# Inverting the heads' triangular matrices as 32x32 blocks: four packed levels and one corner level instead of five 64x64 levels

## The reference

```
def step(state, inp):
    r_t, w_t, k_t, v_t, a_t, b_t = inp
    sa = jnp.einsum('bhvk,bhk->bhv', state, a_t)
    state = state * w_t[:, :, None, :] + sa[..., None] * b_t[:, :, None, :] + v_t[..., None] * k_t[:, :, None, :]
    y = jnp.einsum('bhvk,bhk->bhv', state, r_t)
    return state, y
```

## Time and profile before

| | |
|---|---|
| Median of 3 runs | 3258.43 us (3256.69 to 3261.16) |
| Span of the profiled execution, first to last instruction | 3254.1 us, 4.3 us under the median |
| Stage of the heads, in that span | from about 2330 to 2832 us |
| Its 8 merges | 25.5 to 26.9 us each |
| PE busy over the span | 3029.2 us, 93% |

### The profile page before, as it was taken

How to read it: one execution, slowest core, us unless ns; L and a number is a source line. 1 busy time by engine, 2 the same in 40 slices (tenths; PEclk the granted TensorE clock), 3 DMA queues, 4 the chain that set the end, 5 groups by cost and what they waited for, 6 DMA issues and landing times. The chain is left out here.

```text
span 3254.1 us, 59877 instructions
## 1 busy us (share of the span) xinstructions
PE 3029.2 (93%) x25454; PEld 2407.3 (74%) x25454; DVE 1840.2 (57%) x2665; ACT 1393.4 (43%) x2369; POOL 669.5 (21%) x542
## 2 busy tenths in 40 slices
PE   8989999999978999999989999989788989699999
PEld 6757788887746788887658888767577777588887
DVE  6665533445665543445665736474376867457464
ACT  5555322235455422234464424345465655344242
POOL 1000311211000311212001101133275746011010
PEclk9989999999999999999999999989899999899999
DMA  4101333222101322322012323235411111133232
GB/s 148 52 2 67 103 97 97 92 96 84 52 5 64 99 95 94 97 94 77 1 53 92 109 84 101 88 107 192 142 48 30 49 36 42 48 97 108 80 98 83
DMA packets 82344, 260.72 MB, mean 80 GB/s; under 512 B 9632, under 2 KB 13216, under 8 KB 81824
## 3 DMA queue, kind: packets, MB, share of 16 engines
q1 hardware_dynamic: 71424, 235.39, 22.6%
q10 hardware_dynamic: 10656, 21.50, 1.7%
HBM read 235.89 MB, written 20.97 MB: 79 GB/s over the span
## 5 line engine op out<-in xcount | busy, mean ns | idle before, releaser
L1696 DVE TENSOR_TENSOR mlp_w_lo<-mlp_ring,mlp_w_hi 128x1024 fp32r<-128x1024 f32 (+1 forms) x211 | 251.7, 1193 | 576.8 <-ACT mlp_w_hi L1673 576.7
L1673 ACT ACTIVATE mlp_w_hi<-mlp_ring 128x1024 fp32r<-128x1024 f32 (+1 forms) x211 | 213.2, 1011 | 646.1 <-PE ps L1634 639.2
L1696 DVE TENSOR_TENSOR ffn_w_lo<-ffn_ring,ffn_w_hi 128x1024 fp32r<-128x1024 f32 (+3 forms) x172 | 224.1, 1303 | 443.0 <-ACT ffn_w_hi L1673 443.0
L1673 ACT ACTIVATE ffn_w_hi<-ffn_ring 128x1024 fp32r<-128x1024 f32 (+3 forms) x172 | 187.2, 1089 | 485.9 <-PE ps L1634 480.2
L1633 PE MATMUL ps<-mlp_more_parts,mlp_w_hi 128*128 128x512 f32 x952 | 373.1, 392 | 0.0
L1632 PE MATMUL ps<-tiles_parts,mlp_w_hi 128*128 128x512 f32 x832 | 329.7, 396 | 1.1 <-issue 1.1
L1632 PE MATMUL ps<-ffn_x_parts,ffn_w_hi 128*128 128x512 f32 x792 | 312.4, 395 | 17.8 <-DVE ffn_x_parts L2411 14.2
L1634 PE MATMUL ps<-tiles_parts,mlp_w_lo 128*128 128x512 f32 x832 | 327.7, 394 | 0.0
L1632 PE MATMUL ps<-mlp_more_parts,mlp_w_hi 128*128 128x512 f32 x760 | 305.4, 402 | 21.0 <-DVE mlp_w_lo L1696 12.6
L1633 PE MATMUL ps<-ffn_x_parts,ffn_w_hi 128*128 128x512 f32 x792 | 309.9, 391 | 0.0
L1634 PE MATMUL ps<-ffn_x_parts,ffn_w_lo 128*128 128x512 f32 x792 | 309.9, 391 | 0.0
(11 more groups left out here) (504 smaller groups left out, 6166.2 us busy)
## 6 DMA issues: line engine op xcount, KB each, us to landing
ffn_ring<-in_w_ffn_up SPq DMA_DIRECT2D x88, 512.0 KB, 3.5
mlp_ring<-in_w_up SPq DMA_DIRECT2D x64, 512.0 KB, 3.6
mlp_ring<-in_w_down SPq DMA_DIRECT2D x64, 512.0 KB, 3.5
rwkv_keep<-ffn_ring ACTq DMA_DIRECT2D x64, 256.0 KB, 2.4
sq<-rwkv_keep SPq DMA_DIRECT2D x64, 256.0 KB, 3.1
ffn_ring<-in_w_ffn_down SPq DMA_DIRECT2D x16, 768.0 KB, 4.3
in_ring<-in_w_in SPq DMA_DIRECT2D x22, 512.0 KB, 3.6
mlp_ring<-in_w_in SPq DMA_DIRECT2D x22, 512.0 KB, 3.5
```

The lines of the kernel that those rows point to most:

```text
L1673: nc.scalar.activation(w.w_hi[:, n % SPLIT, 0:width], w.ring[:, n % RING, 0:width], ACT.Copy).then_inc(s["w_hi_ready"], 1)
L1696: nc.vector.tensor_tensor(w.w_lo[:, n % SPLIT, 0:width], w.ring[:, n % RING, 0:width], w.w_hi[:, n % SPLIT, 0:width].bitcast(F32), ALU.sub ...
```

## The change

A 64x64 triangular matrix is cut into two 32x32 diagonal blocks and the 32x32 corner between them. The four first levels work on the diagonal blocks alone. A block's 32 columns are the same columns of the buffers for both blocks, so that `X`, `XT`, `T1` and `NM` are 32 columns wide for each instance (128x128 for each `t`, before 128x256). For that `gram_a` writes rows 32 to 63 of each chunk with their column halves exchanged (`swapped`), so that the own block always stands in columns 0 to 31 of `M0` and the corner of the odd rows in columns 32 to 63. Each of the four levels has `inner` and `outer` of 16 matmul calls of 32x32 instead of 8 of 64x64. The fifth level is one 32x32 corner for each chunk and instance: 8 calls of 32x32 for `inner`, straight from `M0`, and 8 for `outer`. A new buffer `XF` of full width takes the result: POOL puts the diagonal blocks into it (`place`, with a mask), and ACT copies the corner into it in two instructions. `wt` and `u0` read `XF`. The half of `gram_a` that makes `M0` has 16 calls with 32 columns of weights instead of 8 with 64. POOL makes a `part` for four levels instead of five, on 128x128.

```diff
+BW = HD // 2
-RW_LEVELS = 5
+RW_LEVELS = 4
...
-    for level in range(RW_LEVELS):
+    for level in range(RW_LEVELS + 1):
         for tt in range(2):
             order.append((tt, level, False))
...
-        X = sb("X", [P, NT, 4, HD])
-        XT = sb("XT", [P, NT, 4, HD])
-        T1 = sb("T1", [P, 2, 4, HD])
-        NM = sb("NM", [P, PARTS_AHEAD, 4, HD])
+        X = sb("X", [P, NT, 4, BW])
+        XT = sb("XT", [P, NT, 4, BW])
+        XF = sb("XF", [P, NT, 4, HD])
+        T1 = sb("T1", [P, 2, 4, BW])
+        NM = sb("NM", [P, PARTS_AHEAD, 4, BW])
...
-                    for k in range(2):
-                        for d in range(2):
+                    for d in range(2):
+                        for odd in range(2):
                             for hh, u in diagonals():
...
+                                own = slice(at.start + odd * BW, at.start + (odd + 1) * BW)
+                                rhs = BK[lo, c % 2, 0, d, at]
+                                nc.tensor.matmul(m.ps[on, 4 + hh, packed(d)], A[lo, d, own], swapped(rhs) if odd else rhs, start=True, stop=True,
+                                                 skip_group_check=True)
...
                     for i in range(4):
-                        for chunk in (half(0), half(1)):
-                            mm = nc.tensor.matmul(m.ps[chunk, t % 2, packed(i)], NM[chunk, u % PARTS_AHEAD, i, :], XT[chunk, t, i, :],
+                        if level == RW_LEVELS:
+                            for chunk in range(2):
+                                odd = block_of(chunk, 1)
+                                mm = nc.tensor.matmul(m.ps[block_of(chunk, 0), t % 2, narrow(i)], M0[odd, t, i, BW:HD], XT[odd, t, i, :],
+                                                      start=True, stop=True, skip_group_check=True)
+                            continue
+                        for b in range(4):
+                            on = narrow(b)
+                            mm = nc.tensor.matmul(m.ps[on, t % 2, narrow(i)], NM[on, n % PARTS_AHEAD, i, :], XT[on, t, i, :],
                                                   start=True, stop=True, skip_group_check=True)
...
+                        for b in range(4):
+                            on = narrow(b)
+                            mm = nc.tensor.matmul(m.ps[on, 2 + t, narrow(i)], X[on, t, i, :], T1[on, t % 2, i, :],
                                                   start=False, stop=True, skip_group_check=True)
...
+                    act.wait_ge(s["placed"], 4 * c + t + 1)
+                    for chunk in range(2):
+                        on = block_of(chunk, 0)
+                        nc.scalar.activation(XF[on, t, :, BW:HD], m.ps[on, 2 + t, narrow(4, 4)].rearrange("p (i n) -> p i n", i=4), ACT.Copy).then_inc(s["xf_taken"], 1)
...
+                def place(c, t):
+                    pool.wait_ge(s["xt_taken"], within(c, t, RW_LEVELS - 1) + 1)
+                    own = XT[:, t, :, :].unsqueeze(2).broadcast_to([P, 4, 2, BW])
+                    where = mask("place").rearrange("p (h n) -> p h n", h=2).unsqueeze(1).broadcast_to([P, 4, 2, BW])
+                    nc.gpsimd.tensor_tensor(XF[:, t, :, :].rearrange("p i (h n) -> p i h n", h=2), own, where, ALU.mult).then_inc(s["placed"], 1)
```

More of the change, by code:

```diff
@@ L72 @@
 BANDS2_W = 3 * P
-RMASKS, RMASKS_W = columns(("after", HD), ("before", HD), ("upto", HD), ("pair", HD), ("eye", HD), ("merge", RW_LEVELS * HD))
+RMASKS, RMASKS_W = columns(("after", HD), ("before", HD), ("upto", HD), ("place", HD), ("pair", BW), ("eye", BW), ("merge", RW_LEVELS * BW))
 def constants():
@@ L121, in table @@
     def table(name, ones, level=0):
-        r[:, RMASKS[name] + level * HD:RMASKS[name] + (level + 1) * HD] = ones
-    table("after", i > j)
+        width = ones.shape[1]
+        r[:, RMASKS[name] + level * width:RMASKS[name] + (level + 1) * width] = ones
     table("before", i < j)
     table("upto", i <= j)
+    odd, other = i // BW == 1, j // BW == 1
+    table("place", odd == other)
+    i, j = i % BW, j % BW
+    table("after", np.where(other, odd, i > j))
+    j = j[:, :BW]
     table("pair", (i // 2 == j // 2) & (i > j))
@@ L2636, in unit, with within @@
             return 20 * c + 4 * level + t
+        def within(c, t, level):
+            return 16 * c + 4 * level + t
         iterations = range(-1, DT + 2)
@@ L2801, in seed @@
                         pe.wait_ge(s["bonus_ready"], c + 1)
[L2802 removed]
+                    nc.tensor.matmul(m.ps[:, 2 + t, narrow(0, 4)], m.ident, flat(XT[:, t, :, :]), start=True, stop=True).then_inc(s["seeded"], 1)
                 def inner(c, t, level):
[L2805 to L2806 removed]
+                    u, n = unit(c, t, level), within(c, t, level)
+                    if level < RW_LEVELS:
+                        pe.wait_ge(s["nm_ready"], n + 1)
                     if level == 0 and t == 0:
@@ L3132, in _ @@
                             x0(i, t)
-                    parts = [(t, level) for _, t, level, second in merge_order() if not second]
+                    parts = [(t, level) for _, t, level, second in merge_order() if not second and level < RW_LEVELS]
                     for t, level in parts[:PARTS_EARLY]:
@@ L3137, in _ @@
                     parts = iter(parts[PARTS_EARLY:])
-                    for k, _, _, second in merge_order():
+                    for k, t, level, second in merge_order():
                         more = None if second else next(parts, None)
@@ L3141, in _ @@
                             part(i, *more)
+                        if main and level == RW_LEVELS and not second:
+                            place(i, t)
                         scale_beat(i + 1, k)
@@ L3172, in x_turned @@
                 def x_turned(c, t, level):
-                    dve.wait_ge(s["xt_taken"], unit(c, t, level) + 1)
+                    dve.wait_ge(s["xt_taken"], within(c, t, level) + 1)
                     nc.vector.transpose(flat(X[:, t, :, :]), flat(XT[:, t, :, :])).then_inc(s["x_turned"], 1)
@@ L3329, in _ @@
                     for k, t, level, second in merge_order():
-                        if main and second and level < RW_LEVELS - 1:
+                        if main and second and level < RW_LEVELS:
                             x_turned(i, t, level)
```

66 lines of the change are left out of this document (41 added, 25 removed).

## The result

The changed kernel takes 3364.4 us in the median of 4 runs (3360.5 to 3368.2), the kernel before 3257.6 us on the same chip (4 runs, 3253.9 to 3261.2). The ratio is 1.0323, with a 95% interval of 1.031 to 1.0337: some 105 us slower. Forecast were 3339 us within 3300 to 3378, so sign, mechanism and range held, and the size was 25 us short.

A forecast was written before the change was run, and what follows sets the result against it. Instruction supply to PE was taken as the bound: five steady intervals +43.0 us, seventh +10.2, first +8.7, last stretch +11.1, first seeds -0.8, clock +8, together +80 us, giving 3339 us within 3300 to 3378.

The forecast's parts named there:

- The instructions: Merge and gram_a: 1024 + 128 = 1152 more PE instructions an iteration, 4.5 packets; 239 packets in all instead of 203.
- The supply as the bound: PE in the merge waits for its instructions, fed 256 at a time, one such packet in 3.75 us.
- The dense stretch: From the merge's start to the last `turn`: 15.4 packets instead of 10.9, 56.1 us instead of 46.7, +9.4 us.
- The formula: Time from merge start to last `turn`: 14.4 packets at 3.75 us plus one at PE's own 2.1 us, 56.1 us.
- The start with a gain: At the merge's start the instruction buffer is full, so one packet passes at PE's own pace, 2.1 us.
- The clock: Behind the merge, `wt`, `u0` and `sum_outputs` run partly at the lower clock: 1 us an interval (0 to 3), +8 in all.
- The other dense stretches: Outside the five steady intervals: first interval +8.7 us, seventh +10.2, last merge and what follows it +11.1.
- Seeds: Between the last `turn` and the next merge, moving operands fall from 256 to 128 columns: 0.8 us less each time.
- Work inside the stretch: In the merge, a new unit's 32 records start within 0.27 us; PE's savings and 2.3 us of tiling changes are hidden.
- That the supply isn't the bound: Rival: in the merge PE runs ahead and DVE decides, 2.8 us saved a steady iteration, 3231 us; chance 0.04.
- A deeper buffer: Rival: between merges one packet more is buffered, each of 8 stretches 3.75 us shorter, 3309 us; chance 0.10.
- The clock that stays low behind the merge: Rival: the part between last `turn` and next merge is slow too, 6 us of passes double, 3381 us; chance 0.11.

The follow-up runs named there:

- the doses: The changed kernel with 512 more, 512 fewer or 1024 fewer PE instructions an iteration, by adding or leaving out small calls: 3416.9, 3296.7 and 3262.2 us.
- the added calls: The changed kernel with four more one-column 32x32 calls in each inner and outer of levels 0 to 3: 3416.9 us, ratio 1.049.

## Why the prediction was right, and what was off

*The instructions.* Right to the packet: 1152 an iteration, 239 packets.

*The supply as the bound.* Right. The stalls stand 256 instructions apart, the time follows the number of instructions in the doses down to where DVE binds, and neither the columns nor a higher clock changes it. What the runs don't show is why a packet takes so long; the profile has the queue's packets, but not what starts one.

*The dense stretch.* This is the term that was mis-sized. The formula gave 56.1 us. The five steady iterations take 349.83 us (2425.09 to 2774.92), 70.0 each, and 9.6 of it is the sparse stretch with the margins of the earlier trace rows, so 60.4 are left: 4.3 more than forecast.

In the merge (35.1 us by the formula, 37.8 measured) the step that was off is the time of a packet. 3.75 us was called the fastest that PE is fed, but it is the mean of three counts, of 5, 5 and 7 packets in a window, where one packet more or less moves the result by some 0.5 us. Measured from stall to stall, a packet takes 3.90 us, and 4.52 where transfers run. With 4.0, the mean of all 58, the formula gives 2.1 + 8.8 x 4.0 = 37.3 us. The start with a gain was right: up to the end of the first stall the five merges take 3.8 us in the mean for 343 records, 11 ns each, where a packet of 251 in 4.0 us is 16 ns. Waits for DVE or ACT aren't what lengthens a packet: the windows of 4.55 and 4.97 us shown above hold none. They have a DMA share of 0.50 and 0.37, against 0.02 in the shorter ones. The profile counts q8's packets and the transfers' against the same 16 DMA engines, so that the one may well delay the other, but no run moved a transfer, and it stays an association, seen in this run and in the one with 4 columns to move.

Behind the merge the formula has 21.0 us (5.6 packets of 3.75), and 22.6 were measured (the five windows' mean of 22.8, less 0.2 of margin). There the supply isn't the bound: PE is busy for 21.02 of 22.02 us, and the stalls of "issue" are 0 to 1.5 us in such a stretch, 0.7 in the mean of the five. The stretch had 20.4 us before, and `gram_a`'s 8 more calls for each `t` and their changes of tiling run in the open here.

*The clock.* It did fall, to a granted 0.50, the lower of the two levels (1.2 GHz), in most of the merge, and to 0.86 to 0.89 behind it. No run shows the 1 us an iteration that was put down for it there, and none excludes it. Part of the 1.6 us above may be it.

*The other dense stretches.* The first interval grew by 11.8 us (8.7 forecast), the seventh by 12.9 (10.2), the five steady ones by 64.4 (43.0), the last merge and what follows by 17.6 (11.1). Their sum is 106.6; the first merge begins 1.9 us earlier (0.8 forecast), and the spans are 104.6 apart, where the sum had 80 with its 8 for the clock. What follows the last merge grew from 43.26 to 47.53 us, though no instruction was added there. With 4 columns to move it is 45.4, with wide work 45.1. Part of it may be the granted clock of 0.72, against 0.84 in the same stretch before; I leave it open.

*Seeds.* 0.83 us less in the sparse stretch (10.48 to 9.65 above), 0.8 forecast.

*Work inside the stretch.* The small calls started 13.5 ns apart at the lower clock (0.42 us in 31). At a merge's start, at 1.00, 64 records take 0.75 us at 2495.47 us, 8.3 ns from one to the next ((0.75 - 0.23) / 63), as forecast. Under the cover neither counts. That DVE, ACT and POOL would have slack held: ACT's 93.4 us of waiting for `outer` are it.

*The rivals.* That the supply isn't the bound fell with the 65 stalls. The Trainium skill, Runtime: NRT & Kernel Launch, Instruction fetch mechanics, has room for 2048 instructions and calls the crossing of a block mostly hidden; all doses here disagree, since 512 instructions, two blocks, already cost 7.7 us in each merge. A deeper buffer fell with eight stalls in a merge of 2465 records, 9.8 packets with its waits. The clock that stays low behind the merge fell with the sparse stretch's granted clock of 1.00. And half of the calls give 3262 us, not 3231: where the supply is gone as a bound, DVE and the chain leave nothing of the shorter work to be had.

## What to carry to other kernels

Count PE's instructions, not its columns: a 32-bit call is four of them whatever its size, and cutting one 64x64 call into two 32x32 calls halves the array's work and doubles what must be fetched. If "issue" stalls stand a fixed number of records apart, divide the dense stretch's records by that number, multiply by the spacing of the stalls, and compare it with the busy time of the other engines before anything is split. Take the spacing from stall to stall, at several places, and look at the DMA share beside it: a count of a few packets in a window was too coarse here.

## What the runs showed that was not expected

- A wait that is long satisfied isn't free on PE: an instruction that holds two of them took 79 to 97 ns, five to seven times the supply's 14.6 ns for an instruction.
- Wide work that kept PE busy for 6 to 7 us more in a merge of 38 us raised its granted clock from 0.60 to 0.86 and made the merge some 2 us longer, not shorter. What lowered the clock is open: with the added calls PE was busy for 37.6 of 45.3 us, as large a share as with wide work, at a clock of 0.53 to 0.55.
- Packets were slower where transfers ran: 4.52 us in the mean at a DMA share of 0.3 or more, 3.90 at 0.05 or less.
- The price of the same 128 instructions was 23 us in the kernel before and some 10 us in the kernel after.
